# RWKV core: the next pair's raw products in front of the units, and one direction's writes issued by ScalarE

## What is computed

```python
def rwkv7_scan(r, w, k, v, a, b, s0, reverse):
    def step(s, inp):
        rt, wt, kt, vt, at, bt = inp
        sa = jnp.einsum('bhvk,bhk->bhv', s, at)
        s = s * wt[..., None, :] + sa[..., None] * bt[..., None, :] + vt[..., None] * kt[..., None, :]
        return s, jnp.einsum('bhvk,bhk->bhv', s, rt)
...
        kk = kk * lax.rsqrt(jnp.sum(kk * kk, axis=-1, keepdims=True) + 1e-12)
        k = k * (1.0 + (a - 1.0) * k_a)
        return heads(r), heads(decay), heads(k), heads(v), -kk, kk * heads(a), g
...
        y_f, s_f = rwkv7_scan(r, decay[0], k, v, aa, bb, init[0], False)
        y_b, s_b = rwkv7_scan(r, decay[1], k, v, aa, bb, init[1], True)
        return y_f + y_b, (s_f, s_b)
```

## Time and profile before

| | us |
|---|---|
| median of 3 runs | 3207.5 (3188.84 to 3208.7) |
| the profiled execution | 3203.67, span 3202.0 |
| TensorE busy / loads | 2482.0 / 1218.0 |
| VectorE busy | 813.9 |
| ScalarE busy | 479.0 |
| GpSimd busy | 329.4 |
| RWKV core: from pair 0's first raw product to its last VectorE result | about 1988 to 2439 |

### The profile page before, as it was taken

The page is one execution under the profiler, slowest core; times in us unless marked ns, Lnnn a source line. Parts: engine busy times, 40 slices in busy tenths (PEclk is TensorE's granted clock), DMA queues, the critical chain, the costliest instruction groups (busy, mean ns, idle before and its releaser), DMA issues. The chain is left out here.

```text
span 3202.0 us, 41427 instructions
## 1 busy us (share of the span) xinstructions
PE 2482.0 (78%) x18136; PEld 1218.0 (38%) x18136; DVE 813.9 (25%) x1765; ACT 479.0 (15%) x960; POOL 329.4 (10%) x487
## 2 busy tenths in 40 slices
PE   4489995537496888788896896898887788887886
PEld 0134442324243433333332344787775322222222
DVE  1201503455503111111012502566552210000001
ACT  0100003222102000000001102444431100000001
POOL 0000000035101000000001301444440000000000
PEclk9899997769798999999898897999998899899998
DMA  9632110000024699999994224322321899999996
GB/s 378 286 108 79 68 37 1 0 1 1 0 92 159 276 414 403 410 422 421 398 399 202 84 66 134 62 49 51 58 46 61 339 407 403 398 422 422 406 410 276
DMA packets 192005, 692.38 MB, mean 216 GB/s; under 512 B 88952, under 2 KB 124320, under 8 KB 142288
## 3 DMA queue, kind: packets, MB, share of 16 engines
q1 hardware_dynamic: 190704, 689.24, 55.2%
q10 hardware_dynamic: 1120, 0.48, 0.1%
HBM read 675.82 MB, written 13.84 MB: 215 GB/s over the span
## 5 line engine op out<-in xcount | busy, mean ns | idle before, releaser
L1424 PE MATMUL bank<-moe_w,moe_xT 128*64 128x512 f32 (+3 forms) x3072 | 629.5, 566 | 67.5 <-DMA moe_w<-in_exp_w 65.2
L1448 PE MATMUL bank<-moe_w,moe_hidT 128*64 128x512 f32 (+1 forms) x1408 | 383.6, 701 | 132.2 <-DMA moe_w<-in_exp_w 120.7
L1424 PEld LDWEIGHTS bank<-moe_w,moe_xT 128*64 128x64 f32 (+1 forms) x3072 | 197.3, 125 | 505.1 <-issue 402.2
L1448 PEld LDWEIGHTS bank<-moe_w,moe_hidT 128*64 128x64 f32 (+1 forms) x1408 | 111.4, 141 | 369.0 <-issue 219.7
L1516 DVE TENSOR_TENSOR moe_silu<-bank,moe_silu 64x512 f32<-64x512 f32 (+3 forms) x96 | 56.5, 639 | 659.5 <-ACT moe_silu L1479 659.5
L1529 DVE COPY moe_rows<-bank 32x512 f32<-32x512 f32 x96 | 65.9, 686 | 541.5 <-PE bank L1448 540.6
L1479 ACT ACTIVATE moe_silu<-bank 64x512 f32<-64x512 f32 (+3 forms) x96 | 46.2, 546 | 1035.5 <-PE bank L1424 1035.5
L402 PE MATMUL bank<-w_slab,mixT 128*128 128x512 f32 x384 | 166.2, 594 | 1.8 <-PE bank L402 1.5
L1558 POOL TENSOR_TENSOR moe_xn<-moe_xn,moe_w 128x1024 f32<-128x1024 f32 x6 | 18.1, 3021 | 1435.7 <-ACT moe_w L1495 1435.7
L399 PE MATMUL bank<-mixT,w_slab 128*128 128x512 f32 x320 | 140.5, 601 | 10.6 <-DMA w_slab<-in_ab_w_in 9.6
L1678 PE MATMUL bank<-mixture,rw_slab 128*128 128x512 f32 (+1 forms) x384 | 143.6, 527 | 4.5 <-PE bank L1678 3.7
(11 more groups left out here) (468 smaller groups left out, 2999.5 us busy)
## 6 DMA issues: line engine op xcount, KB each, us to landing
moe_w<-in_exp_w SPq DMA_DIRECT2D x256, 1408.0 KB, 14.0
moe_w<-in_exp_w SPq DMA_DIRECT2D x64, 2048.0 KB, 18.6
ada_slab<-in_ada_w SPq DMA_DIRECT2D x32, 1536.0 KB, 12.8
moe_w<-in_exp_w SPq DMA_DIRECT2D x32, 1536.0 KB, 7.2
w_slab<-in_ab_w_in SPq DMA_DIRECT2D x11, 2048.0 KB, 7.7
wo_slab<-in_ab_w_out SPq DMA_DIRECT2D x16, 512.0 KB, 3.5
x_inv_and_t<-x_blocks SPq DMA_DIRECT2D x32, 256.0 KB, 5.1
rw_slab<-in_rw_wk SPq DMA_DIRECT2D x4, 1024.0 KB, 7.1
```

The costliest lines, as they stand in the source:

```text
L1424: mm = pe.matmul(g.ps[k][64 * m:64 * m + M, 0:hi - lo], xg[:, i % 2, j, c, :], wa[:, sl, m, r, lo:hi], start=(c == 0), stop=(c == DC - 1))
L1448: mm = pe.matmul(g.ps[5 + m][64 * m:64 * m + M, :], hidt[:, c, :], wb[:, sl, c - lo, 512 * m:512 * m + 512], start=(c == 0), stop=(c == FC ...
```

## The change

Six moves in the hand-written orders, nothing added to or taken from the arithmetic.

- TensorE: `products(i + 1)` in front of `pmm(i, 0)` instead of behind the last `xmm(i, n)`.
- VectorE: `keys(i + 2)` right behind the sums of pair `i + 2`, at the end of iteration `i`, instead of `keys(i + 1)` between the chain's states; `hats(i + 1, 1)` right behind `hats(i + 1, 0)` instead of behind the fourth addition of the units; `back(i + 1)` in front of the units instead of behind them.
- ScalarE: `raw(i + 1, 0)` and `raw(i + 1, 1)` in front of the units' copies instead of behind, and between the two, from ScalarE itself, the two transfers that write `nt0` to memory (`sent`). SyncE no longer issues these.
- GpSimd: `n_levels` behind the inversion of the blocks instead of in front of it.

The diff, cut to its core:

```diff
@@ sync
-                    W(sp, "nt", i, 2, 1)
-                    for h in range(2):
-                        sp.dma_start(by_row(nscr[0], h, NP, LC), nt[0][HALF[h], :, :]).then_inc(S["nwritten"], 16)
                     W(sp, "n1", i, 1, 1)
@@ gpsimd
-                    if i:
-                        W(pool, "pmm", i - 1, NU, NU)
-                    for d in range(2):
-                        W(pool, "nt", i, 2, d + 1)
-                        for lv in range(2):
-                            pool.tensor_tensor(nlev[d][:, lv, :, :], nt[d][:, :, :], many(g.lev[:, d, lv, :], NCH), ALU.mult).then_inc(S["nlev"], 1)
                     W(pool, "nblock", i, 32, 32)
...
                     pool.tensor_copy(yt[:, 1, :, :], yt[:, 0, :, :].rearrange("p s t -> p t s")).then_inc(S["xblock"], 1)
+                    if i:
+                        W(pool, "pmm", i - 1, NU, NU)
+                    for d in range(2):
+                        W(pool, "nt", i, 2, d + 1)
+                        for lv in range(2):
+                            pool.tensor_tensor(nlev[d][:, lv, :, :], nt[d][:, :, :], many(g.lev[:, d, lv, :], NCH), ALU.mult).then_inc(S["nlev"], 1)
@@ vector
                 sums(1, 1)
+                keys(1)
                 for i in range(DC):
...
-                    if nxt:
-                        keys(i + 1)
                     if prev:
                         state(i - 1, 4)
...
                         hats(i + 1, 0)
+                        hats(i + 1, 1)
                     if prev:
                         mean(i - 1)
+                    if nxt:
+                        back(i + 1)
                     for n in range(NU):
                         xadd(i, n)
...
-                        if nxt and n == 3:
-                            hats(i + 1, 1)
                         if prev and n == 5:
                             gated(i - 1)
-                    if nxt:
-                        back(i + 1)
...
                         sums(i + 2, 1)
+                        keys(i + 2)
@@ scalar
+                def sent(i):
+                    if i:
+                        W(act, "nblock", i - 1, 32, 32)
+                    W(act, "nt", i, 2, 1)
+                    for h in range(2):
+                        act.dma_start(by_row(nscr[0], h, NP, LC), nt[0][HALF[h], :, :]).then_inc(S["nwritten"], 16)
...
                 raw(0, 0)
+                sent(0)
                 raw(0, 1)
...
                     nkv(i, 1)
+                    if nxt:
+                        raw(i + 1, 0)
+                        sent(i + 1)
+                        raw(i + 1, 1)
                     for n in range(NU):
                         product(i, n)
...
-                    if nxt:
-                        raw(i + 1, 0)
-                        raw(i + 1, 1)
@@ tensor
+                    if nxt:
+                        products(i + 1)
                     pmm(i, 0)
...
-                    if nxt:
-                        products(i + 1)
                     solved(i, 0)
```

## The result

The changed kernel takes 3176.5 us (median of 11 runs, 3170.8 to 3185.4), the kernel before 3207.0 us in the same comparison (11 runs, 3188.8 to 3213.7). Between the medians lie 30.5 us, where 37 us were forecast. The ratio of the two kernels is 0.992 with a 95% interval of 0.990 to 0.993, so the gain is 0.8% of the time. By the bound of 1% that the prediction set, that counts as no change, if only just; the interval itself excludes 1.

What follows compares the result with a forecast made beforehand. The RWKV core was taken to be bound by TensorE's wait for each pair's inverse (41.8 us in 8 waits). Savings of 24.9, 3.8, 7.0 and 1.0 sum to 36.7, say 37 us, off 3207.5: forecast 3170 us, range 3153 to 3190.

Steps and rivals of the forecast that it cites:

- the hats' rival: Wait for the hats is 3.5 us, always followed by 1.7 us lost at half speed: 23 us gained, 3184 us; chance 0.17.
- Six pairs: From pair 0's solve to pair 6's: 49.5 us a pair instead of 53.65, six times 4.15, 24.9 us saved.
- The wait for the hats: New TensorE wait before the raw products, until VectorE has made both hats: 2.2 us a pair.
- the clock behind the wait: Slow TensorE clock after the 2.2 us wait for the hats: 0.7 us a pair, between nothing and 1.7.
- ScalarE's issues: Two write issues between the raw copies on ScalarE, ahead of the units' first copy: 0.4 us a pair, bounds 0 and 1.3.
- The key steps: Four VectorE steps leave the stretch between the chain's states: 1.3 of their 2.0 us a pair given back to TensorE.
- the meetings' rival: Key steps collide with GpSimd's level products, up to 1.6 us a pair instead of 0.4: 3179 us; chance 0.12.
- Start: Up to pair 0's solve, pair 1's raw products move into the 7.67 us wait before pair 0's units: 3.8 us saved.
- End: From pair 6's solve to pair 7's units: 27.6 us instead of 34.6, 7.0 us saved.
- Last units and rest: The last units are slow for less long: 1.0 us saved.
- The spare time before the inverse's use: Inverse ready 42.5 us after its raw products, asked for after 49.5 + 2.9: 9.9 us to spare.
- The slower case: GpSimd's inversion stretched from 14.3 to 36 us beside VectorE, binding beyond 24 us: 3226 us; chance 0.05.

Runs made afterwards that it cites:

- a filler: Changed kernel with idle TensorE multiplications in the wait for the hats of pairs 2 to 7: 56 small 3173.1 us, 2 large 3174.6, 36 small 3171.6.
- the run: Changed kernel with GpSimd's inversion of the blocks done twice for pairs 1 to 7: 3192.1 us, ratio 0.996.
- the faster orders: Changed kernel with raw products inside the units, 3165.8 us; its variants: diagonals first 3151.6 (one run), combined 3158.1, loads held until the inverse landed 3167.6.

## Why the prediction was right, and where its sum was off

The mechanism held in all its steps: TensorE no longer waits for the inverse, a wait for the hats stands there instead, the stall in the units is gone, the keys left the chain. The run with the products behind the units shows that their place carries 23 of the core's 29 us. The sum gave 36.7 us, the core 29.2, which is nearer to the 23 of the hats' rival than to the sum. Of the signs, a pair of 49 to 50 us was missed by half a microsecond, and the inverse lands 16 to 18 us ahead of its use instead of some 10.

- Six pairs: 24.9 forecast, 18.75 measured, or 50.5 us a pair instead of 49.5. The missing 6.2 us are three terms. Products and units with their extras were put at 2.9 + 10.0 + 0.7 + 0.4 = 14.0 us and took 14.69 on average: 4.1 us. The wait for the hats was put at 2.2 and took 2.46: 1.6 us. From the solve to the outputs' end 33.3 was forecast and 33.4 measured, one stop of 1.6 us included: 0.5 us.
- Of these the mis-sized term is the clock behind the wait. I took 0.7 us because of two waits in the expert stage, one followed by full speed and one not the earlier trace rows, that is, a chance of less than one half. Where it falls it costs 1.55 us (products and units take 14.83 us instead of 13.28), and it fell in five of the six pairs of the changed kernel, in four of six with SyncE's writes and in all six with the keys between the states. The nearest rows were in the same place of the core, behind the waits for the inverse. Not each of these was followed by slow work, as the prediction has it: before pair 6, which isn't among its rows, the wait of 3.02 us was followed by full speed.

```profile
2352.69 1.15 PE L2280 MATMUL bank<-x_inv_and_t,n_levels 64*64 64x64 f32 x32 [3.02 <-DMA x_inv_and_t<-x_blocks]
```

But in seven of the eight pairs the clock fell. Seven eighths of 1.7 us are 1.5, and with that the term would have been close to the 1.3 that five falls in six cost. The Trainium skill (TensorE: Matmul & The Clock Gate, Part 1) says that the same kernel can get its full clock at another point in each run. No kernel was traced twice here; what the traces show is that within one kernel the same wait of 2.4 us has both outcomes.

- The units themselves take 10.43 us at full rate without any wait, not 10.0: taking the whole of 1.7 and 0.76 off 12.5 was 0.4 too much. Pair 6 of the kernel before, at full clock, had it: 11.17 us to its raw products, less the 0.76.
- ScalarE's issues, 0.4 forecast: nothing where the clock fell, a wait of 0.94 us in the one pair where it didn't, and 0.4 to 0.5 a pair where a filler keeps it full. So this term and that of the clock don't add up: where the one is paid the other isn't. The key steps, 1.3 us a pair: 1.2 when undone. In their new place, where 0.4 was set aside for a meeting with the level products, the first of them takes 1.26 us instead of 0.47 in two of the six pairs and all else in them runs undisturbed; in the pair of the rows above the diagonals end at 2206.1 and the keys start at 2207.8. What GpSimd meets there are the sums. So the meetings' rival (3179 us) did not come about.
- Start: 3.8 forecast, 3.3 measured; pair 1's products start 39.2 us after pair 0's instead of 37.3, behind level products of 5.9 us where I had 5.0. End: 7.0 forecast, 5.6 measured; a stop of 1.84 us in pair 7's token turns is more than the difference. Last units and rest: 1.0 forecast, 1.6 measured.
- The spare time before the inverse's use, 9.9 us, was at least 12.6 in the middle pairs by the run and 16.0 to 18.4 by the trace. I had taken over the 42.5 us path of the kernel before unchanged. From the products to the inversion it is now 10.4 us instead of 12.5, the inversion 12.2 instead of 14.3, and the way out and back 13.1 instead of 15.7; why each is shorter wasn't tried.
- The hats' rival (3184 us) had both of its halves half right: the wait was 2.5 instead of 3.5 us, the clock fell in five pairs of six instead of in all. The slower case would have needed an inversion stretched to 24 us; it took 12.2.
- The chance of 0.62 for faster by over 1% was too high for a sum that lay 5 us beyond that bound: the clock term alone, 0 to 1.7 us in six pairs, was worth more than this margin.

## What to carry to other kernels

When a wait is made shorter, price what stands behind it at the clock that rows at the same place show, all of them and not a choice, and not at that of rows elsewhere: here a wait of 2.4 us cost 1.55 us more in most pairs. When a producer must be ahead of its consumer by a fixed path, put it not only early enough but where its own operands are ready without waiting; inside the consumer's work it gave 19 us more than in front of it. A gain beside the bound has to be costed together with the step that lifts the bound: the keys gave 7 us with the products in front of the units and showed nothing with them behind. The same holds for a cost, since the two issues on ScalarE were free only as long as the clock was slow.

## What the runs showed of the hardware

TensorE can stand still for 0.5 to 1.9 us in a stream of small multiplications with "issue" as the only reason in the profile, that is, without waiting for an engine or a transfer of the kernel. All 34 such stops of these traces end 2.3 to 3.0 us after a transfer of 16 KB on the instruction queue began. The median distance of these transfers over the six pairs is 4.0 to 5.2 us in the 14 kernels, and the ones ahead of a stop come 4.8 to 8.2 us after their predecessor. The reading that fits is that TensorE ran out of instructions because their transfer had to pass DMA engines that were full. It isn't shown: behind six such late transfers in the changed kernel's six pairs there is one stop of over 0.5 us. Taking 640 KB of input loads a pair away brought the stops of six pairs from 5.2 to 0.6 us. In the kernel before there is next to nothing of them (0.2 us), in the changed one 1.8 us show in the six pairs and 1.8 at the end, in the faster orders 3 to 6. I had not expected that a core made faster by removing waits would pay a part of it back there.

TensorE's granted clock fell behind waits of 2.4 to 2.7 us for the hats in 15 of 18 pairs of three kernels (the changed one, the one with SyncE's writes and the one with the keys between the states), and in none of the 18 pairs of the three kernels with fillers of 2.0 to 3.4 us in that place.
